# First mixer: masked copies of the second halves alone, over both banks at once, and the queries' rope part copied by ScalarE

## The reference, cut to what matters

```python
def first_block(x, ...):
    u = rmsnorm(h, mix_norm[layer])
    z = jnp.einsum('bld,de->ble', u, w_in[e])
    hq, hf, hi, hg, cq, ckv, kr = jnp.split(z, IN_SPLITS, axis=-1)
    o_a = hgrn2_mixer(hq, hf, hi, hg, ...)
    o_b = mla_mixer(cq, ckv, kr, ...)
    mix = jnp.einsum('ble,ed->bld', jnp.concatenate([o_a, o_b], axis=-1), w_out[e])
...
def step(S, inp):                      # branch a, one chunk of 64 tokens
    qi, ki, vi, gi = inp
    b = jnp.cumsum(gi, axis=2)
    o_inter = jnp.einsum('bhtk,bhkv->bhtv', qi * jnp.exp(b), S)
    diff = b[:, :, :, None, :] - b[:, :, None, :, :]
    dec = jnp.exp(jnp.where(tri, diff, -jnp.inf))
    att = jnp.einsum('bhtk,bhtsk,bhsk->bhts', qi, dec, ki)
    o_intra = jnp.einsum('bhts,bhsv->bhtv', att, vi)
...
q = jnp.einsum('blr,re->ble', rmsnorm(cq, qa_g), w_q_up)     # branch b: 4 heads of 128 + 64
q = rope_tail(rmsnorm(q, qn_g), cos, sin)                    # the 64 are the rope part
k = rope_tail(rmsnorm(k, kn_g), cos, sin)
o = block_causal_attention(q, k, v, cid)
```

## Time and profile before

| | us |
|---|---|
| median of three runs | 1263.34 |
| profiled execution, span from first to last instruction | 1261.9 |
| PE busy | 1231.6 (98%) |
| DVE busy | 908.1 (72%) |
| ACT busy | 737.1 (58%) |
| POOL busy | 6.4 (1%) |

### The profile page before, as it was taken

One profiled execution on the slowest core, in us unless ns is written; L12 is line 12 of the kernel. 1 busy time (PEld: TensorE's weight loads), 2 busy tenths in 40 slices (PEclk: granted clock), 3 DMA queues, 4 the chain that ended last, 5 costly groups with the idle time before them and its releaser, 6 DMA issues.

```text
span 1261.9 us, 24318 instructions
## 1 busy us (share of the span) xinstructions
PE 1231.6 (98%) x10110; PEld 1206.4 (96%) x10110; DVE 908.1 (72%) x1571; ACT 737.1 (58%) x1257; POOL 6.4 (1%) x16
## 2 busy tenths in 40 slices
PE   8999999999999999999999999999999999999997
PEld 8889799999999999999999999999888899999997
DVE  6896566665446776444876899966788768999656
ACT  6753456664445765334555666655766866665655
POOL 1000000000000000000000000000000000000000
PEclk9999999999999999999999999999899999999999
DMA  7223244555552655553663666574364236665640
GB/s 275 72 101 105 64 164 148 192 181 180 174 168 98 216 186 185 184 184 126 218 195 119 193 194 199 159 238 134 120 225 159 89 117 192 193 189 188 215 141 34
DMA packets 59753, 205.51 MB, mean 163 GB/s; under 512 B 6739, under 2 KB 9340, under 8 KB 59516
## 3 DMA queue, kind: packets, MB, share of 16 engines
q1 hardware_dynamic: 57536, 201.21, 49.0%
q10 hardware_dynamic: 2108, 2.75, 0.7%
HBM read 202.87 MB, written 1.06 MB: 162 GB/s over the span
## 4 chain that ended last, share of the span: by engine, by line
PE 85%; DVE 8%; ACT 4%; issue 1%; DMA 1%; DVEq 0%; ACTq 0%
PE PS L368 69%; PE PS L413 6%; DVE WL L353 2%; PE PS L380 2%; DMA RAW<-wpack 1%; ACT WH L346 1%; PE PS L462 1%; PE PS L2450 1%; ACT EE L2608 1%; PE PS L520 1%; PE PS L2517 0%; PE PS L688 0%; DVE X L1905 0%; ACT L532 0%; PE PS L402 0%
## 5 line engine op out<-in xcount | busy, mean ns | idle before, releaser
L353 DVE TENSOR_TENSOR WL<-RAW,WH 128x1024 fp32r<-128x1024 f32 (+2 forms) x387 | 460.6, 1195 | 211.3 <-ACT WH L346 210.8
L346 ACT ACTIVATE WH<-RAW 128x1024 fp32r<-128x1024 f32 (+2 forms) x387 | 392.3, 1033 | 218.6 <-PE PS L368 184.8
L368 PE MATMUL PS<-UH,WH 128*128 128x256 f32 (+1 forms) x1464 | 415.7, 284 | 7.6 <-DVE WL L353 3.8
L368 PE MATMUL PS<-UL,WH 128*128 128x256 f32 (+1 forms) x1464 | 414.9, 283 | 0.0
L368 PE MATMUL PS<-UH,WL 128*128 128x256 f32 (+1 forms) x1464 | 414.7, 283 | 0.0
L368 PEld LDWEIGHTS PS<-UH,WH 128*128 128x128 f32 x1464 | 276.6, 189 | 8.6 <-issue 3.4
L368 PEld LDWEIGHTS PS<-UH,WL 128*128 128x128 f32 x1464 | 276.9, 189 | 0.0
L368 PEld LDWEIGHTS PS<-UL,WH 128*128 128x128 f32 x1464 | 275.2, 188 | 0.0
L368 PE MATMUL PS<-HL,WH 128*128 128x272 f32 (+1 forms) x512 | 145.8, 285 | 0.0
L368 PE MATMUL PS<-HH,WH 128*128 128x272 f32 (+1 forms) x512 | 145.6, 284 | 0.0
L368 PE MATMUL PS<-HH,WL 128*128 128x272 f32 (+1 forms) x512 | 145.4, 284 | 0.0
(11 more groups left out here) (409 smaller groups left out, 2066.1 us busy)
## 6 DMA issues: line engine op xcount, KB each, us to landing
RAW<-wpack SPq DMA_DIRECT2D x361, 512.0 KB, 4.2
RAW<-wpack SPq DMA_DIRECT2D x18, 384.0 KB, 3.5
RAW<-wpack SPq DMA_DIRECT2D x6, 256.0 KB, 2.7
C<-cst SPq DMA_DIRECT2D x1, 1072.0 KB, 5.9
HB<-bias_rows ACTq DMA_DIRECT2D x1, 1024.0 KB, 5.3
out<-X SPq DMA_DIRECT2D x4, 256.0 KB, 2.3
X<-xin ACTq DMA_DIRECT2D x2, 272.0 KB, 6.0
X<-xin SPq DMA_DIRECT2D x2, 272.0 KB, 5.9
```

What stands on the lines that cost most here:

```text
L346: a.e.activation(WH[n % NH][:, 0:w], RAW[n % NR][:, 0:w], ACT.Copy).then_inc(*a.mark("wh", n))
L353: v.e.tensor_tensor(WL[n % NH][:, 0:w], RAW[n % NR][:, 0:w], WH[n % NH][:, 0:w].bitcast(f32), ALU.subtract).then_inc(*v.mark("wl", n))
L368: ins = t.e.matmul(o, part(n, hw, kw, a, b), x(kx), start=first and not i and not p, stop=last and i == len(kcs) - 1 and p == 2)
```

## The change

In `attention(level)` for levels 1 to 6, the two copies of 512 elements become one copy over both banks that takes only the second half of each stretch of 2h columns: again 512 elements per partition, in 512/h runs of h elements. Level 0 stays as it is, and so do the small copies into ATM. The copy of the rope part moves from DVE to ACT, in front of ACT's square of the same banks; QR's event is now `("qn", 1)`, and the four banks are free for `up("kvup", 0)` after ACT's square, `("hsq", "q", 1)`.

```diff
--- before.py
+++ after.py
@@ -774,7 +774,7 @@
                 ins.then_inc(*t.mark("mix", "hr", "o"))
 
             def rotate(key, src, nh):
-                t.wait_ge("gr", key)
+                t.wait_ge(*(("qn", 1) if key == "q" else ("gr", key)))
                 b = banks.take(t, ("rot", key), ("rsin", key), nh)
                 for hh in range(nh):
                     ins = t.e.matmul(PS[0:64, b + hh, 0:T], c("rot", p=64), src[:, hh, :], start=True, stop=True)
@@ -868,7 +868,7 @@
             latent_sums()
             up("qup", 0, [(0, 0), (1, 1)], 128, ("qn",))
             level(2)
-            up("qup", 1, [(0, 0), (1, 1)], 64, ("gr", "q"))
+            up("qup", 1, [(0, 0), (1, 1)], 64, ("hsq", "q", 1))
             level(3)
             spread_columns("l", lambda i, hh: LAT[:, 1, i:i + 1], ("rkv",), 1)
             up("kvup", 0, [(0, 2), (1, 3)], 128, ("kn",))
@@ -982,6 +982,7 @@
             def query_rest():
                 b1 = banks.at["qup", 1]
                 a.wait_ge("mix", "qup", 1)
+                a.e.activation(QR[:, :, :], PS[0:64, b1:b1 + 4, 0:T], ACT.Copy, scale=g("qr", 0, 64)).then_inc(*a.mark("qn", 1))
                 a.e.activation(QRSQ[:, :, :], PS[0:64, b1:b1 + 4, 0:T], ACT.Square).then_inc(*a.mark("hsq", "q", 1))
 
             def value_rows():
@@ -1182,9 +1183,20 @@
                 v.wait_ge("zero", 3)
                 if level:
                     v.wait_ge("att", level - 1)
-                for x in range(2):
-                    src = PS[:, b + x, :].rearrange("p (n t) -> p n t", t=128)
-                    ins = v.e.copy_predicated(ATT[:, 4 * x:4 * x + 4, :], m, src)
+                h = 1 << level >> 1
+                if level == 0:
+                    for x in range(2):
+                        src = PS[:, b + x, :].rearrange("p (n t) -> p n t", t=128)
+                        ins = v.e.copy_predicated(ATT[:, 4 * x:4 * x + 4, :], m, src)
+                else:
+
+                    def second(z):
+                        return z.rearrange("p (n k s) -> p n k s", n=8, s=2 * h)[:, :, :, h:2 * h]
+                    mh = c("lev", 128 * level, 128 * level + 128).bitcast(u32).rearrange("p (k s) -> p k s", s=2 * h)[:, :, h:2 * h]
+                    k, w = mh.shape[1], mh.shape[2]
+                    ins = v.e.copy_predicated(second(ATT[:, :, :].rearrange("p n t -> p (n t)")),
+                                              mh.unsqueeze(1).to_broadcast([128, 8, k, w]),
+                                              second(PS[:, b:b + 2, :].rearrange("p x t -> p (x t)")))
                 if level <= 4:
                     mt = c("lev", 128 * level, 128 * level + 16, 16).bitcast(u32).unsqueeze(1).to_broadcast([16, 4, 16])
                     src = PS[0:16, banks.at["atm", level], 0:64].rearrange("p (n t) -> p n t", t=16)
@@ -1249,12 +1261,6 @@
             def key_roots():
                 v.wait_ge("hroot", "k")
                 v.e.reciprocal(KSC[:, :, :], KSC[:, :, :]).then_inc(*v.mark("hrec", "k"))
-
-            def query_rest():
-                b = banks.at["qup", 1]
-                v.wait_ge("hsq", "q", 1)
-                v.e.tensor_scalar(QR[:, :, :], PS[0:64, b:b + 4, 0:T], g("qr", 0, 64), None, ALU.mult).then_inc(
-                    *v.mark("gr", "q"))
 
             def key_rest():
                 v.wait_ge("mix", "kr", 0)
@@ -1287,7 +1293,7 @@
                 cb = c("cos", p=64).unsqueeze(1).to_broadcast([64, nh, T])
                 sb_ = c("sin", p=64).unsqueeze(1).to_broadcast([64, nh, T])
                 v.wait_ge("c")
-                v.wait_ge("gr", key)
+                v.wait_ge(*(("qn", 1) if key == "q" else ("gr", key)))
                 v.wait_ge("mix", "rot", key)
                 v.e.tensor_tensor(rr, rr, cb, ALU.mult).then_inc(*v.mark("rcos", key))
                 v.wait_ge(*(("hsum", "q") if key == "q" else ("rsum", "q")))
@@ -1389,7 +1395,6 @@
             latent_roots()
             exponents(5)
             dve_split(v, 16)
-            query_rest()
             operands(4)
             attention(4)
             v.wait_ge("op", 4)
```

## The result

The changed kernel takes 1258.63 us, the median of five runs (1258.29 to 1259.75), against 1263.34 of before (five runs, 1262.01 to 1263.54): ratio 0.9968, 95% interval 0.9956 to 0.998. All executions with a span on record, 36 of the changed kernel and 146 of before, put the means at 1259.28 and 1262.48 us: 3.2 us, or 0.25%. Of the chances, that is the case "above the line" of 2.5 us, which had 0.40. Single executions scatter by about 1 us, so a handful of runs could be off by one.

What follows compares the result with a forecast made beforehand. PE, busy for 1231.6 of 1261.9 us, was taken to bound the kernel, gaining only where it idles behind DVE. 1.24 + 1.26 - 0.03 + 0.06 = 2.53 us, taken as 2.5, gave 1260.85 us; range 1260.3 to 1262.3.

Steps and rivals of the forecast that it cites:

- above the line: Whole kernel: a gain above the 2.5 us that a measurement can tell from no change; chance 0.40.
- What bounds the mixer: First mixer: PE is busy for 1231.6 of 1261.9 us, so only its idle stretches can give time.
- three idle pieces: PE's waits for DVE: 1.22 us before up("kvup", 0), 0.49 before values(0, 0), 1.05 before level(5); together 2.76 us.
- The mixer's sum: DVE's lag before level(5): copies 0.62 twice, QR copy 1.26, less 0.03, gives 2.47 us; 2.53 at keys_turned.
- The copies' price in short runs: Masked copies on DVE, levels 1 to 6: 512 elements cost 0.62 us whatever the run length, half of the pair's 1.24.
- my two bounds: Price of one masked copy: 0.62 us at the low end; 1.27 as if each element were read twice, saving nothing.
- KD term: At keys_turned, which starts right after DVE's KD ends: a further gain of 0.06 us.
- doubled price on the path: Rival: short runs out of PSUM cost twice per element, copies save nothing, 1.26 us remains, time 1262.1; chance 0.08.
- ACT last: Rival: ACT's copy nearer 1.5 us makes ACT the last before level(5); gain 2.1 us, time 1261.2; chance 0.05.
- taken up later: Rival: PE runs into another wait behind the first, or the change does nothing; time 1263.3; chance 0.07.
- slower: Rival: each run costs p extra in the copies of levels 1 to 4; at 8 ns the time is 1266.7; chance 0.08.
- The break-even of 4.5 ns a run: Masked copies of levels 1 to 4: the kernel is slower once each run costs 4.5 ns extra.

Runs made afterwards that it cites:

- the other variants of the table above: Six kernels: either half of the change alone, or the changed kernel with masked copies, instruction order or DVE instruction count altered; mean spans 1.45 to 3.50 us under before.
- delayed kernel: The changed kernel with DVE computing the keys three times, so that PE's level(5) is late again; 1263.27 us, ratio to before 1.0001.

## Why the prediction was wrong

**What bounds the mixer** was right. The three idle pieces were one lag of DVE, two of them are gone and the third is 0.57 us on ACT.

**The mixer's sum** was right: 2.47 us at level(5) forecast, 2.50 to 2.54 in five profiles; 2.53 at keys_turned forecast, 2.57 to 2.61. Copies of levels 3 and 4, 0.61 us each; PE at level(5) at the hour worked out, with DVE still the last there. With one half of the change at a time the parts are 1.03 and 1.27 (1.26 forecast for the rope part's copy), and 0.2 us is a wait on ACT's square that only shows when DVE comes early; that I had no such term did no harm, since the same move removes it.

**The copies' price in short runs** was half wrong. I took 0.62 us for all; with runs of one and two it is 1.10. That price lay between my two bounds, 0.62 and 1.27, and at levels 1 and 2, in front of a wait for PE, it was hidden: the idle 1.00 us of DVE where I had 1.95. A level 1 copy much above 0.73 us was one of my own signs of being wrong, and it came, at 1.31. That the path has runs of 4 and 8, and that those cost nothing extra out of PSUM, no row had shown: there I had luck. Memory Cachelines, in "Advanced Engine Details and Errata" of the Trainium skill, asks for every two consecutive elements to be contiguous for best throughput. Here runs of two elements (8 bytes) cost DVE as much as runs of one, and runs of four were free: a cost of gaps is there on DVE too, and pairs were not enough to avoid it.

**ACT** was right: 0.73 us sooner was forecast, 0.71 came, and the extra microsecond on ACT met only idle time.

**From the sum to the time** is where it failed. The step "1261.9 - 2.5 = 1259.4 us of span; with the 1.4 us around it 1260.8" has three faults. The 1.4 us was the median of three runs less the span of another execution; what lies around a span is 2.14 us. Put right, that alone gives 1261.5, further from the measured time. It does not stay as it is: with seven instructions fewer on DVE it became 1.8, a gain of 0.34 us that I had at nothing without a reason. And the three runs of before stood 0.9 us above the mean of 146. From 1260.85 to the changed kernel's mean of 1259.28 are 1.6 us: 0.86 from the level of before, 0.34 from around the span, and 0.36 inside the span. Of the last, 0.06 are the KD term, which I had. The other 0.3 go with less time at half clock, as in the other variants of the table above; whether the change brings that about remains open, and no term of mine had it. The median of the first five runs is another 0.65 us lower by scatter.

**The range** was too narrow for this. It took in the bounds of my terms and left out how far one execution lies from another: three runs within 0.53 us looked like a kernel that repeats to 0.04%, and 146 had spans from 1258.0 to 1263.4. **The rivals**: no doubled price on the path, ACT last but at 0.57 us, nothing taken up later, nothing slower. The break-even of 4.5 ns a run stands against a measured 0.49 us over the 512 runs of level 1, 1 ns each. But level 2 costs the same with 256 runs and level 3 nothing with 128, so the price is not one per run, as that rival had it.

## What to carry to other kernels

Where PE is busy 98% of the time, find the lag of the other engine that its idle pieces have in common, and only price what lies on that lag; the sum in the timeline was exact to 0.1 us here. Pair the starts of the same instructions in two profiles before explaining a difference of two times: it says at once which stretch moved, and a second profile of the same kernel says which of it is scatter. For such masked copies, halve elements rather than join instructions, and keep runs out of PSUM at four float32 or more, the shortest that were free here.

## What the runs showed of the hardware

- A masked copy of 512 elements out of PSUM lasts 0.70 to 0.75 us in runs of four or more, 1.30 to 1.32 in runs of one or two. All three operands have the short runs; that PSUM is the one that costs is argued from the tensor operations in SBUF with runs of one, which last 0.73 us for 544 elements.
- Two masked copies of 512 elements take 1.24 us, one of 1024 takes 1.21.
- ACT's copy out of PSUM with a gain per partition lasts 1.15 us for 64x1088; the square of the same banks, without a gain, 1.05.
- The clock fell to half behind idle pieces of 1.22 us (once in four profiles of before) and of 2.50 us (delayed kernel); it was at half from 8 to 11 us in three of nine profiles; between 897 and 921 us there is a piece at half in all nine, at places that differ between executions of one kernel. The same idle piece of 1.22 us left it at full in the first profile of before. Over the kernels of the table, a mean clock higher by 0.001 goes with a span shorter by about 1 us beyond the mixer (an estimate, from 0.92 against 0.09 us at 0.99418 against 0.99340).
- Time outside the span is 1.8 or 2.14 us, by the number of instructions (DVE's or the whole program's).
